# An encoder layer with a routed expert stage: slots by one-hot products, expert tables from lanes, and a first split that waits for one expert

## What is computed

```python
g_idx = argmax(g_logits)                       # one of 4 groups
top_v, top_i = top_k(e_logits, 2)              # two of the group's 8 experts
wts = g_w * softmax(top_v)
eid = g_idx * 8 + top_i                        # 2304 x 2 assignments, 32 experts
counts = bincount(eid); padded = ceil(counts / 128) * 128
dest = pad_starts[eid] + rank within the expert     # a slot for each assignment
row_tok[dest] = token                          # slots to tokens, blocks of 128 slots
yb = (silu(xb @ w1[e]) * (xb @ w3[e])) @ w2[e] # for each block, e its expert
out[token] += weight * yb
```

## Time and profile before

| | |
|---|---|
| runs, us | 3526.51 median of 3 (3525.28 to 3530.02) |
| profiled execution | 3525.43 us, span 3523.6 us |
| busy | PE 2933.7 (83%), DVE 2308.3 (66%), ACT 1618.4 (46%), POOL 591.1 (17%) |
| routing stage | from 2266.14, its first load |
| totals counted, next VectorE step | 2285.45 |
| expert stage, first product (L2001) | 2372.18 |
| fifth weight piece rounded (L2077) | starts at 2383.67 |
| 96 expert weight loads (L1640) | the last issued at 3301.8 |
| last transposes of the loop (L1992) | 3389.16 |
| combine stage, first load | 3404.45 |

### The profile page before, as it was taken

One profiled execution on the slowest core, in us unless ns is written; L12 is line 12 of the kernel. 1 busy time (PEld: TensorE's weight loads), 2 busy tenths in 40 slices (PEclk: granted clock), 3 DMA queues, 4 the chain that ended last, 5 costly groups with the idle time before them and its releaser, 6 DMA issues. The chain is left out here.

```text
span 3523.6 us, 42543 instructions
## 1 busy us (share of the span) xinstructions
PE 2933.7 (83%) x12997; PEld 2003.0 (57%) x12997; DVE 2308.3 (66%) x2869; ACT 1618.4 (46%) x2029; POOL 591.1 (17%) x431
## 2 busy tenths in 40 slices
PE   6999999669999999996992899719999999999940
PEld 3666666424444444444661677507777777777730
DVE  2555555437777777764776544448888888887856
ACT  2323323103333333345551323117877777877754
POOL 0000000000000000005990000042222222222225
PEclk8999999769999999998995899859999999999975
DMA  6112111451110111000006233345677876578347
GB/s 242 49 45 63 48 45 51 138 165 27 37 33 21 36 36 33 21 16 4 0 0 221 95 126 126 116 162 205 221 260 262 290 256 233 215 261 304 141 152 315
DMA packets 239082, 446.29 MB, mean 127 GB/s; under 512 B 22689, under 2 KB 96509, under 8 KB 238253
## 3 DMA queue, kind: packets, MB, share of 16 engines
q1 hardware_dynamic: 222429, 397.68, 33.6%
q0 software_dynamic: 16592, 47.84, 3.8%
HBM read 367.46 MB, written 86.40 MB: 129 GB/s over the span
## 5 line engine op out<-in xcount | busy, mean ns | idle before, releaser
L2142 DVE TENSOR_TENSOR weights_rest<-w,weights_rounded 128x2048 fp32r<-128x2048 f32 x314 | 716.4, 2289 | 191.3 <-ACT weights_rounded L2077 191.2
L2077 ACT ACTIVATE weights_rounded<-w 128x2048 fp32r x314 | 598.0, 1913 | 148.9 <-PE ps_up L2001 94.2
L837 ACT ACTIVATE probs<-ps_scores 128x1024 f32<-128x1024 f32 x260 | 266.5, 1025 | 502.8 <-PE ps_scores L768 415.1
L860 DVE TENSOR_REDUCE part_max<-ps_max 128x1 f32<-128x512 f32 (+1 forms) x528 | 337.9, 678 | 193.1 <-PE ps_max L745 193.0
L2001 PE MATMUL ps_up<-weights_rounded,block_T_rounded 128*128 128x512 f32 x832 | 339.3, 408 | 28.6 <-DVE weights_rest L2142 24.0
L430 PE MATMUL ps_proj<-w_in,n1T 128*128 128x512 f32 (+2 forms) x1152 | 348.5, 460 | 6.5 <-PEq L108 6.5
L2001 PE MATMUL ps_up<-weights_rounded,block_T_rest 128*128 128x512 f32 x832 | 327.1, 393 | 0.0
L2001 PE MATMUL ps_up<-weights_rest,block_T_rounded 128*128 128x512 f32 x832 | 325.8, 392 | 0.0
L778 PE MATMUL ps_attn<-probs,v 128*64 128x512 f32 x1040 | 283.6, 625 | 0.0
L430 PEld LDWEIGHTS ps_proj<-w_in,n1T 128*128 128x128 f32 x1152 | 197.5, 192 | 145.7 <-issue 130.9
L745 PE MATMUL ps_max<-kT,q_for_max 128*128 128x512 f32 (+1 forms) x528 | 191.0, 435 | 76.1 <-DVE part_max L860 41.4
(11 more groups left out here) (345 smaller groups left out, 5022.9 us busy)
## 6 DMA issues: line engine op xcount, KB each, us to landing
w<-in_w SPq DMA_DIRECT2D x96, 2048.0 KB, 10.6
expert_rows<-scratch_y SPq DMA_DIRECT2D x36, 512.0 KB, 9.8
w_ada_rest<-in_w_ada SPq DMA_DIRECT2D x5, 2048.0 KB, 15.6
scratch_qT<-qT_stage SPq DMA_DIRECT2D x18, 512.0 KB, 3.5
q_for_max<-scratch_qT SPq DMA_DIRECT2D x36, 256.0 KB, 5.7
q_rounded_twice<-scratch_qT SPq DMA_DIRECT2D x36, 256.0 KB, 4.4
mix_rows<-scratch_mix SPq DMA_DIRECT2D x18, 512.0 KB, 5.0
scratch_h<-h_rows SPq DMA_DIRECT2D x18, 512.0 KB, 2.6
```

The costliest lines, as they stand in the source:

```text
L837: act.activation(pf[:, slot(p, n), :], ps_s[:, n % 2, :], ACT.Exp).then_inc(exp_done, 1)
L860: nc.vector.tensor_reduce(mx[:, p, n // H, n % H:n % H + 1], ps_m[:, n % 2, 0:PART], AX.X, ALU.max).then_inc(m_taken, 1)
L2077: act.activation(split_piece(wh, s), raw_piece(s, buf[0]), ACT.Copy).then_inc(hi_done, 1)
L2142: nc.vector.tensor_tensor(split_piece(wl, s), raw_piece(s, buf), split_piece(wh, s).bitcast(F32), ALU.subtract).then_inc(lo_done, 1)
```

## The change

Routing first reduces the totals over the tiles directly and makes the tables before the slots. Each expert table is computed with one entry per lane (`per_lane`, `columns`): lane r compares the 32 experts with its own number. Three products with the identity turn the columns into rows of PSUM (`ps_w`); TensorE does them ahead of the modulation products. `turn_expert` and `first_block` are written, on one partition, in the middle of the 18 sums. SyncE then loads the first expert alone; the second expert's loads are the first thing that it does in the expert stage.

A slot table is made on chip: for each k VectorE writes a one-hot of the row (18 x 128 numbers a lane) and of the block (18 x 72), GpSimd multiplies the latter by the assignment's number, and 36 products sum them up in PSUM (`ps_i`), from which VectorE makes token and result row (empty slots come out as the sentinel). The indirect stores, the table in DRAM, its filling and reading back go away. The constant table grows by 128 numbers a row. The modulation row is added on VectorE behind the one-hots and stored from ScalarE's queue; the combine stage waits for it. In the expert stage the first piece waits for `up_in[0]` alone, and the pieces 0 and 1 are split ahead of block 0's halves. The turns without an expert wait one more step, for which VectorE gives `up_split` and `down_split` one more at its end.

```diff
@@ -174,13 +174,8 @@
         @block.gpsimd
         def _(gp):
             gp.memset(S["eps"][:, :], EPS).then_inc(zeroed, 1)
-            gp.memset(S["empty_slots"][:, :, 0], 0).then_inc(zeroed, 1)
-            gp.memset(S["empty_slots"][:, :, 1], 2 * T).then_inc(zeroed, 1)
-            gp.wait_ge(zeroed, 3)
+            gp.wait_ge(zeroed, 1)
             gp.memset(S["kT1"][HD:HD + 1, :, :].bitcast(F32), 1.0).then_inc(zeroed, 1)
-            gp.wait_ge(zeroed, 4)
-            gp.dma_start(R["row_ids"].rearrange("(p b) o -> p b o", p=P), S["empty_slots"][:, :, :]).then_inc(zero_out, 16)
-            gp.wait_ge(zero_out, 16)
@@ route_phase @@
...
+        def over_tokens(a):
+            return a.rearrange("p (o n) -> p o n", o=1).to_broadcast([P, NT, a.shape[1]])
+        def each_token(a, n):
+            return a.rearrange("p (t o) -> p t o", o=1).to_broadcast([P, NT, n])
...
-            for j in range(2):
-                e = sp.value_load(S["turn_expert"][0:1, j:j + 1], min_val=0, max_val=NE - 1)
-                load_weights(sp, I, S, e, j, ("w1", "w3"), S["up_in"][j])
-                load_weights(sp, I, S, e, j, ("w2",), S["down_in"][j])
-            for j in range(NJ):
-                sp.wait_ge(mod_done, j + 1)
-                sp.dma_start(R["mod"][:, mod_cols(MOD_LAST, j)], mrow[side_rows(j), :]).then_inc(mod_out, 16)
-            sp.wait_ge(mod_out, 16 * NJ)
+            e = sp.value_load(S["turn_expert"][0:1, 0:1], min_val=0, max_val=NE - 1)
+            load_weights(sp, I, S, e, 0, ("w1", "w3"), S["up_in"][0])
+            load_weights(sp, I, S, e, 0, ("w2",), S["down_in"][0])
-                gp.iota(ids[:, k, :, 0], [[P, NT]], base=0, channel_multiplier=1).then_inc(ids_ready, 1)
-                gp.iota(ids[:, k, :, 1], [[P, NT]], base=k * T, channel_multiplier=1).then_inc(ids_ready, 1)
+                gp.iota(ids[:, k, :], [[P, NT]], base=k * T + 1, channel_multiplier=1).then_inc(ids_ready, 1)
+            gp.iota(lane_int[:, :], [[0, 1]], base=0, channel_multiplier=1).then_inc(ids_ready, 1)
+            gp.wait_ge(ids_ready, 3)
+            gp.tensor_copy(lane[:, :], lane_int[:, :]).then_inc(lane_ready, 1)
+            gp.tensor_copy(idf[:, :, :], ids[:, :, :]).then_inc(ids_ready, 1)
             gp.wait_ge(ids_ready, 4)
-            gp.wait_ge(slots_ready, 2)
-            for t in range(NT):
-                for k in range(2):
-                    gp.indirect_dma_start(R["row_ids"], bass.IndirectOffsetOnAxis(ap=S["slots"][:, k, t:t + 1], axis=0),
-                                          ids[:, k, t, :], None).then_inc(scattered, 16)
-            gp.wait_ge(scattered, 16 * 2 * NT)
+            for k in range(2):
+                gp.wait_ge(block_one_hot, k + 1)
+                gp.tensor_tensor(at_block[:, k], at_block[:, k], each_token(idf[:, k, :], MB), ALU.mult).then_inc(block_ready, 1)
...
@@ -1724,6 +1729,9 @@
             act.activation(gk[:, 3], gk[:, 2], ACT.Exp).then_inc(act_s, 1)
             act.wait_ge(both, 2)
             act.activation(g1[:, 6, :], g1[:, 5, :], ACT.Exp).then_inc(act_s, 1)
+            for j in range(NJ):
+                act.wait_ge(mod_done, j + 1)
+                act.dma_start(R["mod"][:, mod_cols(MOD_LAST, j)], S["mod_last"][side_rows(j), :]).then_inc(S["mod_out"], 16)
         @block.tensor
         def _(pe):
@@ -1734,11 +1742,21 @@
                 nc.tensor.matmul(ps_r[:, n, 0:HT * NE], rank_w[:, :], part, start=True, stop=True)
                 last = nc.tensor.matmul(ps_t[:, n, 0:HT * NE], ones[:, :], part, start=True, stop=True)
             last.then_inc(counted, 1)
+            pe.wait_ge(columns_ready, 1)
+            for n in range(3):
+                last = nc.tensor.matmul(ps_w[0:1, n * P:(n + 1) * P], columns[:, n:n + 1], S["ident"][:, :], start=(n == 0), stop=(n == 2),
+                                        skip_group_check=True)
+            last.then_inc(rows_ready, 1)
             pe.wait_ge(ada_in, 32 * NJ)
             for k in range(KC):
                 for j in range(NJ):
                     last = nc.tensor.matmul(ps_g[side_rows(j), :], S["csilu"][:, k, :], wada[:, j, k, :], start=(k == 0), stop=(k == KC - 1))
             last.then_inc(mod_ready, 1)
+            for n, (k, t) in enumerate(itertools.product(range(2), range(NT))):
+                pe.wait_ge(row_ready, k + 1)
+                pe.wait_ge(block_ready, k + 1)
+                last = nc.tensor.matmul(ps_i[:, 0:MB], at_row[:, k, t, :], at_block[:, k, t, :], start=(n == 0), stop=(n == 2 * NT - 1))
+            last.then_inc(slots_ready, 1)
         @block.vector
         def _(dve):
@@ -1788,16 +1806,45 @@
             L(V.tensor_tensor(S["weights"][:, 1, :], S["weights"][:, 0, :], g1[:, 6, :], ALU.mult))
             dve.wait_ge(counted, 1)
-            L(V.memset(pre[:, 0, :], 0.0))
-            for t in range(NT):
-                L(V.tensor_tensor(pre[:, t + 1, :], pre[:, t, :], ps_t[:, t // HT, (t % HT) * NE:(t % HT + 1) * NE], ALU.add))
-            L(V.tensor_scalar(ex[:, 0, :], pre[:, NT, :], float(P - 1), None, ALU.add))
+            for n in range(2):
+                last = V.tensor_reduce(ex[:, n, :], ps_t[:, n, 0:HT * NE].rearrange("p (c e) -> p e c", e=NE), AX.X, ALU.add)
+            L(last)
+            L(V.scalar_tensor_tensor(ex[:, 0, :], ex[:, 0, :], float(P - 1), ex[:, 1, :], ALU.add, ALU.add))
             L(V.tensor_copy(exi[:, 0, :], ex[:, 0, :]))
             L(V.tensor_scalar(exi[:, 1, :], exi[:, 0, :], int(math.log2(P)), None, ALU.arith_shift_right))
             L(V.tensor_copy(ex[:, 1, :], exi[:, 1, :]))
+            V.tensor_scalar(fl[:, 0, :], ex[:, 1, :], 0.0, None, ALU.is_gt)
             L(V.tensor_tensor_scan(ex[:, 2, :], ones[:, 0:NE], ex[:, 1, :], 0.0, ALU.mult, ALU.add))
-            L(V.tensor_tensor(ex[:, 3, :], ex[:, 2, :], ex[:, 1, :], ALU.subtract))
-            L(V.tensor_scalar(ex[:, 4, :], ex[:, 3, :], float(P), None, ALU.mult))
+            V.tensor_scalar(ex[:, 5, :], ex[:, 2, :], 1.0, None, ALU.add)
+            V.tensor_tensor(ex[:, 3, :], ex[:, 2, :], ex[:, 1, :], ALU.subtract)
+            L(V.tensor_tensor_scan(fl[:, 1, :], ones[:, 0:NE], fl[:, 0, :], 0.0, ALU.mult, ALU.add))
+            V.tensor_scalar(ex[:, 4, :], ex[:, 3, :], float(P), None, ALU.mult)
+            V.tensor_copy(exi[:, 0, :], ex[:, 5, :])
+            L(V.tensor_tensor(fl[:, 2, :], fl[:, 1, :], fl[:, 0, :], ALU.subtract))
+            V.tensor_scalar(S["first_block"][:, NE:2 * NE], exi[:, 0, :], 1, None, ALU.arith_shift_right)
+            L(V.scalar_tensor_tensor(fl[:, 3, :], fl[:, 2, :], 1.0, fl[:, 0, :], ALU.add, ALU.mult))
+            V.tensor_copy(ex[:, 5, :], S["first_block"][:, NE:2 * NE])
+            L(V.tensor_scalar(fl[:, 4, :], fl[:, 3, :], -1.0, None, ALU.add))
+            number = tables[:, 12:12 + NE]
+            dve.wait_ge(lane_ready, 1)
+            V.tensor_scalar(columns[:, 3:4], ex[:, 5, NE - 1:NE], 2.0, 1.0, ALU.mult, ALU.add)
+            V.scalar_tensor_tensor(per_lane[:, 0, :], fl[:, 4, :], lane[:, 0:1], number, ALU.is_equal, ALU.mult)
+            V.scalar_tensor_tensor(per_lane[:, 1, :], fl[:, 4, :], lane[:, 0:1], ex[:, 3, :], ALU.is_equal, ALU.mult)
+            L(V.scalar_tensor_tensor(per_lane[:, 2, :], ex[:, 2, :], lane[:, 0:1], fl[:, 0, :], ALU.is_le, ALU.mult))
+            V.tensor_scalar(columns[:, 3:4], lane[:, 0:1], fl[:, 1, NE - 1:NE], columns[:, 3:4], ALU.is_ge, ALU.mult)
+            L(V.tensor_reduce(columns[:, 0:3], per_lane[:, :, :], AX.X, ALU.add))
+            V.tensor_scalar(columns[:, 2:3], columns[:, 2:3], float(NE - 1), None, ALU.min)
+            V.tensor_tensor(columns[:, 1:2], columns[:, 1:2], columns[:, 3:4], ALU.add).then_inc(columns_ready, 1)
+            L(V.memset(pre[:, 0, :], 0.0))
+            for t in range(NT // 2):
+                L(V.tensor_tensor(pre[:, t + 1, :], pre[:, t, :], ps_t[:, t // HT, (t % HT) * NE:(t % HT + 1) * NE], ALU.add))
+            dve.wait_ge(rows_ready, 1)
+            V.tensor_copy(S["turn_expert"][0:1, :], ps_w[0:1, 0:NE])
+            V.tensor_copy(S["first_block"][0:1, 0:NE], ps_w[0:1, P:P + NE]).then_inc(tables_ready, 1)
+            for t in range(NT // 2, NT):
+                L(V.tensor_tensor(pre[:, t + 1, :], pre[:, t, :], ps_t[:, t // HT, (t % HT) * NE:(t % HT + 1) * NE], ALU.add))
             L(V.tensor_tensor(big[:, 4], pre[:, 0:NT, :], ex[:, 4, :].rearrange("p (o e) -> p o e", o=1).to_broadcast([P, NT, NE]), ALU.add))
             for n in range(2):
@@ -1809,57 +1856,37 @@
                 L(V.tensor_reduce(g1[:, 9, :], big[:, 0], AX.X, ALU.add))
                 L(V.tensor_copy(place[:, 0, :], g1[:, 9, :]))
...
+                V.tensor_scalar(place[:, 1, :], place[:, 0, :], int(math.log2(P)), None, ALU.arith_shift_right)
                 L(V.tensor_scalar(place[:, 2, :], place[:, 0, :], P - 1, None, ALU.bitwise_and))
...
+                V.tensor_copy(placef[:, k, 1, :], place[:, 2, :])
```

(43 more changed lines are left out.)

90 lines of the change are left out of this document (28 added, 62 removed).

## The result

The changed kernel takes 3500.24 us (median of 4 runs, 3497.19 to 3500.90) where the kernel before takes 3527.03 (4 runs, 3525.28 to 3530.02): 0.9921 of it, 95% interval 0.9904 to 0.9939. That is 26.8 us less; forecast were 37.9, so the direction was right and the size was not: 3500.2 lies above the upper end, 3497.5. The profiled execution took 3500.52 us, with a span of 3498.7.

What follows compares the result with a forecast made beforehand. Two parallel chains, GpSimd's 36 indirect stores and the expert table with its weight loads, then 13.35 us of prologue, delay the expert loop. First product at 2334.3 instead of 2372.18, 37.9 us earlier, gives 3488.6 us; range 3481.5 to 3497.5.

Steps and rivals of the forecast that it cites:

- the slot products: Routing, TensorE: 18 products of 72 columns per k at 0.24 us each, 4.3 us for the last 18.
- the gather beside the second expert's weights: Expert prologue: gathers start together with the second expert's loads; 0.3 us added, bounded by 0 and 3.
- the loop is untouched: Expert loop: first product to the end stays 1151.4 us; over 2 us longer would make the main step wrong.
- E: End of routing, when the slot table is done; forecast at 2319.8, say 2320 us.
- Expert table: Routing: totals counted at 2285.45, table at 2292.7 us instead of 2318.93, first expert's loads from 2293.7.
- VectorE and GpSimd: Routing's slots: both engines take turns, GpSimd's 2.39 us product coming behind the row one-hot; 34 to 40 us gained, chance 0.50.
- rival (b): Routing's slots: engines don't hold each other, VectorE goes first at k = 1, or clock up; 3482 to 3486 us, chance 0.27.
- Rival (c): Expert prologue: the gather queues behind the second expert's weights, 11.2 us; gain 28.5, 3498 us; chance 0.14.
- The order of the split: Expert prologue: weight pieces 0 and 1 before block 0's halves give 0.65 us only.
- (d): Expert prologue: the first split still waits for expert 1; gain 30 us, about 3496.6; chance 0.03.
- (e): Routing: GpSimd's product runs on a slow path, kernel slower than before; 3537.8 us at 27 us each; chance 0.02.
- Removed GpSimd work at the start: nothing: Program start: the two removed memsets and one store lie beside SyncE's first loads, so worth nothing.

Runs made afterwards that it cites:

- e5: Changed kernel with bf16 one-hots for the slot table, the assignment's number split in two exact parts, twice the products; 3492.50 us in one run.
- e3: Changed kernel, but SyncE waits for the first two gathers to land before issuing the second expert's weights; 3499.51 us.
- e12: Changed kernel with bf16 slot products, VectorE multiplying the block one-hot, both experts' upper matrices loaded from routing on, lower ones after the first gathers; 3487.08 us, 0.9881 of before.
- e7: Changed kernel, but block 0's halves are taken first and weight pieces 0 and 1 behind them, as before the change; 3499.51 us.
- e8: Changed kernel, but the first piece waits for both experts' upper matrices, the second's loads staying in the expert stage; 3505.97 us.
- e6: Changed kernel, but VectorE multiplies the block one-hots itself and GpSimd does nothing there; slot table 35.96 us after the totals, 1.3 earlier than in the changed kernel.
- e1: Changed kernel unaltered, timed again in five rounds with a second profile; 3498.87 us, 0.9915 of before.
- e4: Changed kernel, but both experts' weights are issued in routing, the first split still waiting for the first expert alone; 3495.25 us.
- e10: Changed kernel with the two memsets, the store of empty slots and its wait back in the first stage; routing's first load at 2266.55 us.
- e14: Changed kernel unaltered, run in turn with e13 on one chip; 3488.84 us, routing's first load at 2262.35 us.
- e15: Same kernel as e13, the changed kernel with the first stage restored, in turn with e16; routing's first load at 2267.09 us.
- e13: Changed kernel with the first stage's memsets, store of empty slots and wait restored, second look after e10; routing's first load at 2268.45 us.
- e16: Changed kernel unaltered, third look, run in turn with e15 on one chip; routing's first load at 2271.30 us.
- e11: Kernel before, unaltered, profiled once more; routing's first load at 2267.72 us, 1148.8 us from the first product to the end.

## Why the prediction was right, and where it was wrong

The way to the gain was forecast rightly, its size was not. Two terms of the sum were too small, each inside the bound stated for it: the slot products (4.3 us forecast, 7.9 measured) and the gather beside the second expert's weights (0.3 at the first product, 2.2 measured). These two were taken apart by experiments. Alone they would have made some 3493 us, which is inside the range. What carried the median to 3500.24, past 3497.5, are the parts that the sum put at nothing and gave no width: the stages ahead of routing and all that lies behind the first product ("the loop is untouched"). Their cause is only in part known.

**Bound, and what the change is worth.** Right: both chains that ended near 2356 are gone, no store by row numbers is left, and the whole gain is made between routing's first load and the first product. E to copy took 1.37 (forecast 1.3), ScalarE began at E + 3.1 (2.8), VectorE's rests ended at E + 9.7 (9.3).

**Expert table.** Right: 7.25 us after the totals forecast, 7.2 measured (2297.85 against totals at 2290.62), and weights issued 1.0 later. (The table above gives it from routing's first load, where the totals came 0.7 sooner after than before.)

**VectorE and GpSimd.** Right, rival (b) falls: both GpSimd products start on paper with the row one-hots and take 4.53 and 4.61 (forecast 4.95), and VectorE's next product is lengthened from 0.75 to 2.91. The Trainium skill (SBUF — State Buffer, "Who interferes with whom") has the port pair as an exclusive lock for the whole instruction; the trace agrees: GpSimd's result is there 2.2 us after the row one-hot, and VectorE's product ends 0.6 after that. GpSimd's second product was done 27.8 after the totals, 0.7 sooner than forecast.

**Slot products: the first mis-sized term.** The step that failed: "288 columns give 0.96, so 72 give 0.24", taken over 0.46 each for load and product one behind the other. Measured: 7.92 for the last 18, 0.44 each, at a granted clock of 0.50. The rows that the price came from hold the answer: the earlier trace rows count 16 for eight products of 36 columns, and two for one product of 288. An fp32 product stands in the trace as two records, with a weight load each, and the 0.22 per record of the earlier trace rows has to be taken twice. At 36 columns (0.45) and at 72 (0.44) the price is the same, so there the load sets it, not the columns: that is read from these two rows, no run changes the load alone. The forecast had named this as a bound ("were load and product not overlapped, 0.46 each, 8.2"). Cost: 3.6 us; less the 0.7 gained above, and some 0.2 in the last steps, the slot table stood 2.7 later after the totals. e5 shows the term: in bf16, with twice the products, 2.63 instead of 7.92.

**The gather: the second.** The forecast priced the second expert's weights beside the gathers at 0.3 (1.5 hidden), with 3 as its bound. Measured: the first transposes at E + 10.25 instead of E + 6, 4.2 late, of which 1.9 net of that 0.3 (2.2 in all) show at the first product, E + 16.2. e3 and e12 show the cause of 3.3 to 3.4 of the 4.2: with no weights beside it, the wait falls from 5.4 to 2.1 and 2.0. Rival (c) was this mechanism with a price too high (11.2); that its 3498 lies nearest to the median is luck. The Trainium skill (DMA: Bandwidth & Descriptors, "SWDGE vs HWDGE vs iDMA") has each DMA engine go round-robin between the two kinds of queue, which the prediction read as a loss of at most the gather's own length. The trace agrees: from 4.2 us to 8.0 in the middle, a loss of 3.8 against a length of 4.2. The prediction's mistake was to put the middle of the rows of the loop, where gathers run under load but have time, in place of this bound.

**The order of the split.** Forecast 0.65, "since TensorE needs both halves of x anyway"; measured 2.7 (e7). It is worth more just because the gather is late: weights are rounded while the block is still on its way. With an early gather (e12, 12.39 from the copy to the product against 13.35 before) it is 1.0, and 1.7 if counted from the transposes (6.95 against 8.63), since e12's gather is still 0.7 slower than before's.

**Rivals (d) and (e).** e8 shows what the one-expert wait holds off (84.80 instead of 72 to 73), and the rows of L2106 that nothing is waited for in the changed kernel: (d) falls. Its price was too low as well: it had the first piece at E + 18 and the product at E + 22.3; e8 has them at E + 18.0 and E + 28.6, since the block's halves stand behind the weights. Rival (e) falls too: GpSimd's products have the price expected.

**"The loop is untouched".** Wrong by the prediction's own mark of 2 us: 1154.61, and 1152.0 to 1154.6 in four profiles of the changed kernel (mean 1153.7) against a mean of 1150.5 in three of before. The mean 3.1 falls into three parts: 1.8 from the first product to the last store of results (1018.9 before, 1020.7 after), 0.8 in the handover behind it, and 0.5 in the last stage (119.0 and 119.5), where the reason stays open; SyncE's new wait is not it, since the gate rows behind it are read 1.3 us after the stage's first load in both.

The handover runs from the last store of the loop to the first load of the combine stage, and is the same within 0.3 in the three profiles of before and in the four of the changed kernel; before, after, e12:

```profile
3391.81 1.92 POOL L1963 DMA_INDIRECT scratch_y<-expert_y,block_results  x1 [4.72 <-ACT expert_y L2094]
3404.45 0.82 SPq L2235 DMA_DIRECT2D expert_rows<-scratch_y  x2
```
```profile
3365.65 1.93 POOL L1991 DMA_INDIRECT scratch_y<-expert_y,block_results  x1 [4.73 <-ACT expert_y L2123]
3379.08 0.82 SPq L2266 DMA_DIRECT2D expert_rows<-scratch_y  x2
```
```profile
3355.61 1.92 POOL L2008 DMA_INDIRECT scratch_y<-expert_y,block_results  x1 [4.73 <-ACT expert_y L2140]
3368.26 0.82 SPq L2283 DMA_DIRECT2D expert_rows<-scratch_y  x2
```

12.64, 13.43 and 12.65 us. The new last wait of VectorE, priced at nothing, is in e12 too, so it is not that. e6 has 12.63: it differs from the changed kernel only in that GpSimd no longer multiplies in routing, some 1000 us earlier, which e12 shares; every other kernel with these GpSimd products has 13.40 to 13.66. How the one could act on the other stays open.

In the loop there are single steps, mostly of 1.5 to 2.9 us, where TensorE's clock falls. At the thirteenth pair of blocks, some 476 us behind the first product, TensorE waits some 2 us for VectorE's rest of a block in every profile looked at. Windows of 2 us over that gap, before:

```profile
2848.00:2850.00 2.00, 0.37 (x3) 0.37 (x4) 2.00 (x3) 2.00 (x2) 0.00 (x0) 1.00 1.05 412
2850.00:2852.00 2.00, 2.00 (x12) 1.66 (x11) 2.00 (x2) 1.09 (x2) 0.01 (x1) 1.00 1.05 409
```

and in e1:

```profile
2822.00:2824.00 2.00, 0.53 (x4) 0.53 (x5) 2.00 (x3) 2.00 (x2) 0.00 (x0) 0.93 1.03 406
2824.00:2826.00 2.00, 2.00 (x7) 1.61 (x6) 2.00 (x2) 1.02 (x2) 0.39 (x1) 0.50 1.06 414
2826.00:2828.00 2.00, 2.00 (x8) 1.59 (x7) 2.00 (x2) 0.00 (x0) 1.86 (x1) 0.72 1.04 416
```

Same gap, same load; before, TensorE goes on at 2.4 GHz with 12 products in the next 2 us, in e1 at 1.2 GHz with 7. This step is there in ten of the fifteen profiles with the changed loop (the first of after, e1, e4, e5, e8 to e10, e12, e14, e15), and not in e3, e6, e7, e13 and e16 (e16 has one at the tenth pair), nor in the three of before. Another, at the 23rd pair, is in two profiles of before and not in e11 (2.5 to 2.8 us). With one such step each, the way from the first product to the last store takes 1019.6 and 1019.9 us before, 1019.1 in e14 and 1019.7 in e13: as long. Such steps come and go within one kernel; whether the changed kernel meets more of them in the mean (1.8 us) these runs don't settle.

**Ahead of routing.** "Removed GpSimd work at the start: nothing" holds within some 0.5 us up to the first read of the queries near 672 us; whether the kernel's new layout shifts the mean of the later stages by some 2 us is neither shown nor refuted. What was missing is a width for it: the earlier trace rows gave one profile's start of routing as if it were fixed, and it scatters by 11.5 us in the changed kernel. The three parts add up in the means of the profiles (three of before, four of the changed kernel): 33.1 us between routing's first load and the first product (105.57 and 72.43), less 3.1 behind it, less 2.7 ahead, make 27.3, against the measured 26.8 and 29.3 (e1). e14, at 3488.84, meets the forecast of 3488.6 with both mis-sized terms in it: luck, since its routing began 9.7 us earlier than in the first profile of the changed kernel.

## What to carry to other kernels

Before a matmul's price is scaled, count the records against the products in the code: here an fp32 product is two records with a load each, narrow ones (36 and 72 columns) cost the same, and exact small integers split into bf16 parts were cheaper. A prologue's gather that a wait used to keep alone on the DMA has to be repriced together with the transfers that the change starts beside it: issue what is needed first, then the gather, then the rest. Where a landmark ahead of the edit scatters by more than the term in dispute, count from a landmark behind it, and look at the same kernel several times before a cause is sought.

## What the runs showed of the hardware that was not expected

- 18 fp32 products of 128x128 with 72 columns take 7.9 us at the lower clock; 36 bf16 products of the same shape 2.6.
- A gather of 128 rows landed in 4.2 us (middle of three) with no weights under way and in 8.0 with 2 MB loads of SyncE's queue beside it. Its waiter waited 5.4 us instead of 1.8, and 2.0 to 2.1 when the loads were held back.
- A gap of 2 us in TensorE's work is answered by the lower clock in some runs and not in others, at the same place of the same code, and mostly costs 1.5 to 2.9 us (0.50 for some 4 us in e1, 1.00 before).
- VectorE multiplies 1296 numbers in 1.51 us; GpSimd's result is there 2.2 us after VectorE's instruction that held it, and VectorE's next product is lengthened from 0.75 to 2.91 meanwhile.
- The changed kernel took 1186.3 to 1194.2 us in four profiles for one and the same stretch, in which nothing had been edited.
